# Cross attention's values computed at the start of a two-layer kernel and kept in DRAM, in place of beside the norm ahead of the queries

## The chip, the cores and the metric

The kernel runs on one core of a Trainium2 chip. The metric is the device time in microseconds (us), the median of several executions. The engines are called PE (TensorE), DVE (VectorE), ACT (ScalarE), POOL (GpSimd) and SP (SyncE, which here only issues DMAs).

## The reference, cut to what matters

Two layers with a conditioning vector, and then a block with its own weights. Its cross attention reads a memory `mem` of 256 tokens by 1024 features that depends on nothing computed before:

```
m  = rms_norm(mem, norm_mem)               # 256 x 1024
kv = m @ w_xkv                             # keys, values: 1024 features each
q  = rms_norm(x, norm_xattn) @ w_xq        # x: 256 latent tokens after the mixing layer
q, k normalised per head of 256 (4 heads), softmax(q k^T), times v, then w_xo, added to x
```

The norm divides every token's row by a root mean square r of that row. So the values of a token are `(mem * norm_mem) @ w_v / r`: the division may come before the product or after it.

The first layer needs `norm(x) * (1 + scale) + shift`, and scale and shift come from a product of the conditioning vectors with the ada weights; so the first feed-forward (called mlp00) can't begin before eight 1 MB pieces of `w_ada` have come and been used.

## The kernel before, in words

Activations stand feature-major: 128 partitions of features, tokens along the free dimension. Every large product is done in fp32r in three matmuls (`three`, L231): both operands are split into a high part and a low part, and lo*hi, hi*lo and hi*hi are added in PSUM. The weights come as 554 units of 128 x 1024 values (512 KB). For each unit SP issues a DMA into one of 3 landing buffers (`load`), ACT copies the high part into one of 4 slots (`feed_act`, L208), POOL subtracts to get the low part (`feed_pool`, L220), and PE uses it. SP's load of unit u waits for the low part of unit u-3, ACT's copy of u for PE's last use of u-4. The order of the units is the list `STREAMS`; the order of everything on an engine is the order in which its program is written, by hand, and semaphores count the steps (`mark`, `after`).

The start (`start_pe`, `start_act`, `start_dve`): PE does the eight ada pieces (`ada_pe`, each 8 products in 4 column groups), ACT squares the tokens (`square_act`, L636), PE sums the squares with a matrix of ones (`stat_pe`, L642), ACT takes the root (L690), DVE the reciprocal, PE spreads it over the partitions (`spread_pe`, L701), DVE multiplies (L729), ACT and DVE split into high and low (L715, L736). SP's order of DMAs: cond_pack, ada 0 and 1, tokens (2 MB), weight units 0 to 2, ada 2 to 7, then units from 3.

Much later the SSD heads run (`ssd_heads_*`): a loop over 16 heads in which PE, ACT, DVE and POOL alternate and PE does the products of conv_out besides. In its steps 11 to 18 ACT also squares one tile of the memory and PE sums it (`mem_square`, `mem_stat`, L2479). Their root and reciprocal go along with those of the SSD norm. In `ssd_out_*` the memory is multiplied by gain and reciprocal and split into mem_hi and mem_lo. Then follow the keys (`cross_k_pe`), the mixing product (`mix_pe`), and `cross_vq_pe`: the values (16 tiles of two 512-column products, 96 matmuls in all), with the sums and the spread of the norm of xattn written between them, and then the queries. The steps of that norm on ACT, DVE and POOL (L690, L729, L715, L763) lie beside the values' matmuls. `QUIET` names the norms in whose gaps no filler matmuls (`busy_pe`, L650) are put. Last come the attention heads (`cross_heads_*`), the output product and the last feed-forward (mlp_up, mlp_down).

During mlp00 ACT issues DMAs of further ada rows (`rows_dma`, L606), which DVE multiplies.

Of the kernel before, what the change touches and what calls it, by code (L numbers as in the profile page):

```python
# [51 lines left out]
class Feed:  # L52
# [12 lines left out]
    def ahead(self, stream, tiles):  # L65
# [6 lines left out]
                  ("ones", (128,))],  # L72
# [6 lines left out]
             ("norm_xattn", (8,)), ("norm_mem", (8,)), ("xattn_gains", (4,)), ("norm_mlp", (8,))],  # L79
}  # L80

STREAMS = ["w_up00", "w_down00", "w_dn", "w_dn_out", "w_up01", "w_down01", "w_up10", "w_down10",
           "w_swa_k", "w_swa_v", "w_swa_q", "w_swa_out", "w_up11", "w_down11",
           "w_glu", "w_gate", "w_k", "w_v", "w_q", "w_z", "w_dt", "w_xbc", "w_attn_out", "w_conv_out", "w_ssd_out", "w_xk", "w_mix",
           "w_xv", "w_xq", "w_xo", "w_mlp_up", "w_mlp_down"]
# [9 lines left out]
class Kit:  # L95
    def __init__(self, nc, ctx, dram, steps, counted):
# [10 lines left out]
        self.mem_landed, self.skewed, self.stored = sem("mem_landed"), sem("skewed"), sem("stored")  # L107
        f = lambda name, *shape, dtype=F32: ctx.enter_context(nc.sbuf_tensor(name, [P, *shape], dtype))
# [17 lines left out]
        self.rms, self.rr = f("rms", 96), f("rr", 96)  # L126
# [11 lines left out]
    def places(self):  # L138
# [12 lines left out]
        self.pieces = f("ada_pieces", 132, 256)  # L151

# [45 lines left out]
        self.mem_sq = f("mem_squares", 13, 2, LAT)  # L198
# [429 lines left out]


def square_act(k, act, st, d, src, ready):  # L630
    tokens = src.shape[-1]
    if ready is not None:
        act.wait_ge(*ready)
    if d >= 2:
        act.wait_ge(*k.PE.after(st, "stat", d - 2))
    k.nc.scalar.activation(k.sq[:, d % 2, 0:tokens], src, ACT.Square).then_inc(*k.AC.mark((st, "sq", d)))  # L636


def stat_pe(k, pe, st, d, tokens, bank=4):
    pe.wait_ge(*k.AC.after(st, "sq", d))  # L640
    for c in range(tokens // P):
        mm = k.nc.tensor.matmul(ck(k.B[bank], c), k.sq[:, d % 2, c * P:(c + 1) * P], k.C["ones"],  # L642
                                start=d == 0 and c == 0, stop=d == KT - 1, skip_group_check=True)
    mm.then_inc(*k.PE.mark((st, "stat", d)))
# [30 lines left out]

def sums_dve(k, dve, st, d, tokens):
# [3 lines left out]
    s, bank = k.sqs[:, 0:tokens], k.B[6 if st == "norm xattn" else 7][:, 0:tokens]  # L680
# [98 lines left out]
def up_freed(k, st):  # L779
    return lambda n: None if n < 4 else (k.DV.after(st, "raw", (n - 4) // 2) if n % 2 else k.AC.after(st, "silu", (n - 4) // 2))  # L780
# [1651 lines left out]
MEM_SQUARES = 10  # L2432
# [3 lines left out]
def ssd_heads_pe(k, pe):  # L2436
# [38 lines left out]
    def mem_stat(d):  # L2475
        pe.wait_ge(*k.AC.after("mem", "sq", d))
        for c in range(2):
            at = 288 + 2 * d + c
            mm = nc.tensor.matmul(k.B[5][:, at:at + 1], k.mem_sq[:, d % 2, blk(c)], k.C["ones"][:, 0:1], start=True, stop=True)  # L2479
        mm.then_inc(*k.PE.mark(("mem", "stat", d)))  # L2480

    for j in range(INNER + 4):
# [8 lines left out]
        if MEM_SQUARES < j <= MEM_SQUARES + KT:  # L2491
            mem_stat(j - 1 - MEM_SQUARES)
# [6 lines left out]
def ssd_heads_act(k, act):  # L2499
# [20 lines left out]
    def mem_square(d):  # L2520
        if d == 0:
            act.wait_ge(k.mem_landed, 16)
        if d >= 2:
            act.wait_ge(*k.PE.after("mem", "stat", d - 2))
        nc.scalar.activation(k.mem_sq[:, d % 2, :], k.mem[:, d, :], ACT.Square).then_inc(*k.AC.mark(("mem", "sq", d)))

    for j in range(INNER + 3):
# [10 lines left out]
        if MEM_SQUARES <= j < MEM_SQUARES + KT:  # L2538
# [948 lines left out]
```

## Time and profile before

| | before |
|---|---|
| median of 3 runs | 2796.22 us (2790.86 to 2797.05) |
| profiled execution, span from first to last instruction | 2797.4 us |
| PE busy | 2734.1 us, 98% |
| PE weight loads | 2393.1 us, 86% |
| DVE busy | 1431.5 us, 51% |
| ACT busy | 1184.1 us, 42% |
| POOL busy | 1470.3 us, 53% |
| mean granted clock of PE | 0.987 |

The profile gives no time of the profiled execution besides its span, so the span stands for it. The page also has the span in 40 slices of 70 us: PE is at 9 tenths or more in all but the first, which has 7. PEclk is the clock that was granted to PE, as a share of 2.4 GHz.

### The profile page before, as it was taken

The numbers are of one execution on the slowest core, as the hardware profiler recorded it, in microseconds if no ns is written. First come the engines' busy times: TensorE is split into PE (matmuls) and PEld (weight loads), VectorE is DVE, ScalarE is ACT, GpSimd is POOL, SyncE is SP. The second block draws the span as 40 slices with busy tenths as digits, with TensorE's granted clock in tenths as the row PEclk, the third lists the DMA queues.
The fourth block names the chain that finished last, engine by engine and source line by source line (L and its number), as shares of the span: only waits on it lengthen the run. The fifth ranks groups of instructions, "written<-read, shape, count | busy, mean of one in ns | idle before, by whom it ended". The sixth has DMA issues, their size and how long they took to land.

```text
span 2797.4 us, 52973 instructions
## 1 busy us (share of the span) xinstructions
PE 2734.1 (98%) x22044; PEld 2393.1 (86%) x22044; DVE 1431.5 (51%) x2755; ACT 1184.1 (42%) x2115; POOL 1470.3 (53%) x809
## 2 busy tenths in 40 slices
PE   7999999999999999999999999999999999999999
PEld 5888888778888888889888896899997898998999
DVE  3777327656654566415666035453184776612560
ACT  3222235335554322223222246544455565555553
POOL 2444434443324444444444442488884576696887
PEclk9999999999999999999999999999998999999999
DMA  6555322310002555434554336365563353354555
GB/s 263 200 200 196 120 90 90 94 46 4 4 26 68 189 181 179 129 98 147 181 187 155 105 96 129 99 196 186 173 188 109 107 157 123 111 177 136 156 190 160
DMA packets 105973, 380.96 MB, mean 136 GB/s; under 512 B 11367, under 2 KB 16648, under 8 KB 104456
## 3 DMA queue, kind: packets, MB, share of 16 engines
q1 hardware_dynamic: 87304, 310.47, 35.5%
q10 hardware_dynamic: 18432, 67.12, 6.9%
q8 instruction: 175, 2.87, 0.4%
q14 instruction: 62, 0.51, 0.1%
HBM read 373.34 MB, written 4.19 MB: 135 GB/s over the span
## 4 chain that ended last, share of the span: by engine, by line
PE 93%; ACT 3%; DVE 2%; issue 1%; POOL 1%; DMA 0%; SPq 0%; ACTq 0%; POOLq 0%
PE bank L233 26%; PE bank L234 25%; PE bank L235 25%; PE bank L1096 2%; PE upper_banks L234 1%; PE upper_banks L1898 1%; PE upper_banks L235 1%; PE upper_banks L233 1%; PE upper_banks L1881 1%; PE bank L1872 1%; PE upper_banks L1073 1%; PE upper_banks L1223 1%; PE bank L1210 1%; PE bank L1106 1%; PE upper_banks L1221 1%
## 5 line engine op out<-in xcount | busy, mean ns | idle before, releaser
L226 POOL TENSOR_TENSOR weights_lo<-weights_landing,weights_hi 128x1024 fp32r<-128x1024 f32 x554 | 1336.5, 2418 | 1175.9 <-ACT weights_hi L216 1175.2
L216 ACT ACTIVATE weights_hi<-weights_landing 128x1024 fp32r<-128x1024 f32 x554 | 587.1, 1061 | 1156.1 <-PE bank L235 1043.0
L233 PE MATMUL bank<-normed_hi,weights_lo 128*128 128x256 f32 (+1 forms) x2776 | 925.2, 333 | 3.4 <-DVE normed_lo L736 2.1
L234 PE MATMUL bank<-normed_lo,weights_hi 128*128 128x256 f32 (+1 forms) x2776 | 918.0, 331 | 0.0
L235 PE MATMUL bank<-normed_hi,weights_hi 128*128 128x256 f32 (+1 forms) x2776 | 917.0, 330 | 0.0
L233 PEld LDWEIGHTS bank<-normed_hi,weights_lo 128*128 128x128 f32 x2776 | 521.6, 188 | 70.0 <-issue 4.4
L235 PEld LDWEIGHTS bank<-normed_hi,weights_hi 128*128 128x128 f32 x2776 | 521.6, 188 | 56.1
L234 PEld LDWEIGHTS bank<-normed_lo,weights_hi 128*128 128x128 f32 x2776 | 521.8, 188 | 55.7
L233 PE MATMUL bank<-hidden_hi,weights_lo 128*128 128x256 f32 (+1 forms) x1026 | 340.5, 332 | 0.0
L234 PE MATMUL bank<-hidden_lo,weights_hi 128*128 128x256 f32 (+1 forms) x1026 | 340.5, 332 | 0.0
L235 PE MATMUL bank<-hidden_hi,weights_hi 128*128 128x256 f32 (+1 forms) x1026 | 340.0, 331 | 0.0
L818 DVE TENSOR_TENSOR hidden_lo<-silus,hidden_hi 128x512 fp32r<-128x512 f32 (+1 forms) x88 | 201.6, 2291 | 88.4 <-ACT hidden_hi L805 88.4
L234 PEld LDWEIGHTS bank<-hidden_lo,weights_hi 128*128 128x128 f32 x1026 | 192.6, 188 | 21.5
L233 PEld LDWEIGHTS bank<-hidden_hi,weights_lo 128*128 128x128 f32 x1026 | 192.6, 188 | 21.2
L235 PEld LDWEIGHTS bank<-hidden_hi,weights_hi 128*128 128x128 f32 x1026 | 192.6, 188 | 21.1
L872 DVE SCALAR_TENSOR_TENSOR residual<-bank,gate,residual 128x256 f32<-128x256 f32 x70 | 31.1, 479 | 331.8 <-PE bank L235 331.8
L620 DVE CUSTOM_DVE_ANT_0 ada_products<-ada_rows,upper_banks,k_cond_pack 128x1024 f32<-128x1024 f32 x128 | 163.2, 1275 | 22.6 <-DMA ada_rows<-w_ada_rows 13.4
L620 DVE CUSTOM_DVE_ANT_0 ada_rows<-ada_rows,upper_banks,k_cond_pack 128x1024 f32<-128x1024 f32 x128 | 163.2, 1275 | 0.0
L816 DVE TENSOR_TENSOR silus<-silus,bank 128x512 f32<-128x512 f32 (+1 forms) x88 | 54.6, 621 | 186.8 <-PE bank L235 151.9
L2111 DVE SCALAR_TENSOR_TENSOR upper_banks<-gl,k_pack,upper_banks 128x255 f32<-128x255 f32 (+14 forms) x240 | 113.4, 473 | 8.2
L867 DVE TENSOR_TENSOR residual<-residual,bank 128x256 f32<-128x256 f32 x24 | 9.9, 417 | 129.8 <-PE bank L235 129.8
L1014 DVE SCALAR_TENSOR_TENSOR dn_convs<-bank,k_pack,dn_convs 128x508 f32<-128x508 f32 (+1 forms) x96 | 71.8, 748 | 3.4
(465 smaller groups left out, 3687.2 us busy)
## 6 DMA issues: line engine op xcount, KB each, us to landing
weights_landing<-w_up SPq DMA_DIRECT2D x176, 512.0 KB, 3.5
ada_rows<-w_ada_rows ACTq DMA_DIRECT2D x128, 512.0 KB, 4.3
weights_landing<-w_down SPq DMA_DIRECT2D x88, 512.0 KB, 3.5
weights_landing<-w_dn SPq DMA_DIRECT2D x33, 512.0 KB, 3.5
weights_landing<-w_mlp_up SPq DMA_DIRECT2D x32, 512.0 KB, 3.5
weights_landing<-w_mlp_down SPq DMA_DIRECT2D x32, 512.0 KB, 3.5
weights_landing<-w_gate SPq DMA_DIRECT2D x24, 512.0 KB, 3.5
weights_landing<-w_xbc SPq DMA_DIRECT2D x24, 512.0 KB, 3.5
```

The lines of the kernel that those rows point to most:

```text
L216: k.nc.scalar.activation(k.WH[:, u % SLOTS, :], k.W[:, u % LANDS, :], ACT.Copy).then_inc(*k.AC.mark(("unit hi", u)))
L226: k.nc.gpsimd.tensor_tensor(k.WL[:, u % SLOTS, :], k.W[:, u % LANDS, :], k.WH[:, u % SLOTS, :].bitcast(F32), ALU.subtract).then_inc(*k.PO. ...
L233: nc.tensor.matmul(out, ll, rh, start=start, stop=False, skip_group_check=True)
L234: nc.tensor.matmul(out, lh, rl, start=False, stop=False, skip_group_check=True)
L235: return nc.tensor.matmul(out, lh, rh, start=False, stop=stop, skip_group_check=True)
L620: nc.vector.tensor_tensor_reduce(k.row[r % ROW_LANDS][:] if c else k.row_out[:], k.row[r % ROW_LANDS][:], k.upper[:, c * D:(c + 1) * D], 1 ...
L816: nc.vector.tensor_tensor(s, s, k.B[(2 * p + 1) % 4][:, 0:tokens], ALU.mult).then_inc(*k.DV.mark((st, "raw", p)))
L818: nc.vector.tensor_tensor(lo(p), s, hi(p).bitcast(F32), ALU.subtract).then_inc(*k.DV.mark((st, "lo", p)))
L872: nc.vector.scalar_tensor_tensor(x, k.B[n % 4][:, a - first:b - first], gate(n, c), x, ALU.mult, ALU.add).then_inc(*k.DV.mark(*([(st, "ev" ...
L1014: nc.vector.scalar_tensor_tensor(y[:, :, a:b], x[:, :, a + shift:b + shift], taps[:, j:j + 1], y[:, :, a:b], ALU.mult, ALU.add).then_inc(* ...
L1096: mm = k.nc.tensor.matmul(bank[block(to), at + c * BLK:at + (c + 1) * BLK], lhs(rows, to, c), rhs(rows, to, c), start=True, stop=True)
L2111: nc.vector.scalar_tensor_tensor(y[:, a:LAT], x[:, 0:LAT - a], w[:, at, j:j + 1], y[:, a:LAT], ALU.mult, ALU.add).then_inc(*k.DV.mark(("co ...
```

## The change

1. The unit stream `w_xv` goes from behind `w_mix` to the very front of `STREAMS`. A copy of the memory is loaded at the start, multiplied by norm_mem (not divided by the root), split in high and low, and the values' products are done between the ada pieces. Squares, sums and root of the memory are done there too. The division by the root is in the eviction from PSUM (`early_v_act`).
2. The values (1 MB) are stored into a DRAM tensor, and loaded again on SP ahead of the second unit of w_xq. ACT's first row DMA of mlp00 waits for the store, since it writes over that place.
3. The memory's statistics leave the SSD heads; the reciprocals `mem_r` kept from the start are used instead. The memory itself is still loaded again for the keys.
4. The tokens' squares at the start are summed by DVE in a bank (`sums_act`, `sums_dve`, `sums_pe`) instead of by 32 matmul blocks on PE (`stat_pe`).
5. The cross stage has no values in it: sums, spread, queries follow on the mixing product directly. `cross_spread_pe` comes after the third tile of the queries instead of the second. The keys' loop is written by tile, in the same order as before.

```diff
-STREAMS = ["w_up00", "w_down00", "w_dn", "w_dn_out", "w_up01", "w_down01", "w_up10", "w_down10",
+STREAMS = ["w_xv", "w_up00", "w_down00", "w_dn", "w_dn_out", "w_up01", "w_down01", "w_up10", "w_down10",
...
+    if st == "mlp00" and p == 0:
+        act.wait_ge(k.v_stored, 16)
...
-        if MEM_SQUARES < j <= MEM_SQUARES + KT:
-            mem_stat(j - 1 - MEM_SQUARES)
...
-        if MEM_SQUARES <= j < MEM_SQUARES + KT:
-            mem_square(j - MEM_SQUARES)
...
-def cross_vq_pe(k, pe):
...
-            if t == 2:
-                sums_pe(k, pe, "norm xattn", LAT)
-            if t == 6:
-                spread_pe(k, pe, "norm xattn", LAT)
-            wv = tile_parts(k, pe, "w_xv", t, 512)
...
+def cross_kq_pe(k, pe):
+
+    sums_pe(k, pe, "norm xattn", LAT)
+    spread_pe(k, pe, "norm xattn", LAT)
     linear(k, pe, "cross q", "w_xq", KT, KT, both2(k), LAT,
-           lambda n: k.AC.after("cross q", "ev", n - 4) if n >= 4 else k.AC.after("cross v", n // 2, n % 2), norm_ready(k, "norm xattn"),
+           lambda n: k.AC.after("cross q", "ev", n - 4) if n >= 4 else k.DV.after("mix", "ev", 4 + n), norm_ready(k, "norm xattn"),
            first=1, beside=lambda n: cross_beside_pe(k, pe, n))
...
+        if x == 0:
+            pe.wait_ge(k.v_loaded, 16)
...
+def early_v_pe(k, pe, u):
+
+    for t in (2 * u, 2 * u + 1):
+        e, d = t // KT, t % KT
+        wv = tile_parts(k, pe, "w_xv", t, 512)
+        if e == 0:
+            pe.wait_ge(*k.DV.after("early mem", "lo", d))
+        for c in range(2):
+            mm = three(k.nc, k.B[2 * e + c][:], [x[:, d, blk(c)] for x in (k.em_hi, k.em_lo)], wv, d == 0, d == KT - 1)
...
 def start_pe(k, pe):
     pe.wait_ge(*k.AC.after("cond"))
+    for u in range(3):
+        early_v_pe(k, pe, u)
+    ada_pe(k, pe, 0)
+    early_v_pe(k, pe, 3)
+    early_stat_pe(k, pe)
+    for u in range(1, 4):
         ada_pe(k, pe, u)
+        early_v_pe(k, pe, 3 + u)
+    ada_turn_pe(k, pe, 3)
+    early_v_pe(k, pe, 7)
+    sums_pe(k, pe, "norm00", TOK)
+    ada_pe(k, pe, 4)
+    spread_pe(k, pe, "norm00", TOK)
+    for u in range(5, ADA_FIRST):
+        ada_pe(k, pe, u)
     ada_turn_pe(k, pe, ADA_FIRST - 1)
...
+def early_v_act(k, act, e):
+    act.wait_ge(*k.PE.after("early v", e))
+    if e == 0:
+        act.wait_ge(*k.DV.after("early mem", "r"))
+    for c in range(2):
+        k.nc.scalar.activation(k.early_v[:, c, e * 512:(e + 1) * 512], k.B[2 * e + c][:], ACT.Identity,
+                               scale=k.mem_r[:, c:c + 1]).then_inc(*k.AC.mark(("early v", e, c)))
...
 def start_act(k, act):
...
+    for d in range(KT):
+        if d % 2 == 0:
+            feed_act(k, act, min(d // 2 + 1, LANDS))
+        if d == 0:
+            act.wait_ge(k.early_mem_landed, 16)
+        nc.scalar.activation(k.em_hi[:, d, :], k.early_mem[:, d, :], ACT.Identity, scale=k.C["norm_mem"][:, d:d + 1]).then_inc(
+            *k.AC.mark(("early mem", "hi", d)))
+    for d in range(KT):
+        nc.scalar.activation(k.early_sq[:, d, :], k.early_mem[:, d, :], ACT.Square).then_inc(*k.AC.mark(("early mem", "sq", d)))
+    feed_act(k, act, 5)
+    act.wait_ge(*k.DV.after("early mem", "sums"))
+    nc.scalar.activation(k.rms[:, 60:62], k.rms[:, 62:64], ACT.Sqrt, scale=1.0 / D, bias=k.C["eps"]).then_inc(*k.AC.mark(("early mem", "rms")))
+    early_v_act(k, act, 0)
+    feed_act(k, act, 7)
+    for u in range(4):
         ada_act(k, act, u)
-    act.wait_ge(k.tokens_landed, 16)
+    feed_act(k, act, 8)
     for d in range(KT):
-        square_act(k, act, "norm00", d, k.X[:, d, :], None)
+        sums_act(k, act, "norm00", d, k.X[:, d, :], (k.tokens_landed, 16))
     rms_act(k, act, "norm00", TOK)
-    feed_act(k, act, LANDS)
-    for u in range(2, ADA_FIRST):
+    early_v_act(k, act, 1)
+    feed_act(k, act, k.F.base["w_up00"] + LANDS)
+    for u in range(4, ADA_FIRST):
         ada_act(k, act, u)
...
+            F.base["w_up00"] + 6: values_out, F.base["w_xq"] + 1: values_in}
     sp.dma_start(k.C["cond_pack"][:], dram["cond_pack"]).then_inc(k.cond_landed, 16)
-    for u in range(2):
+    load(0)
+    sp.dma_start(k.early_mem[:], dram["late_mem"]).then_inc(k.early_mem_landed, 16)
+    load(1)
+    load(2)
+    for u in range(4):
         ada_dma(k, sp, u)
+        load(3 + u)
     sp.dma_start(k.X[:], dram["tokens"]).then_inc(k.tokens_landed, 16)
-    for u in range(LANDS):
-        load(u)
-    for u in range(2, ADA_FIRST):
-        ada_dma(k, sp, u)
-    for u in range(LANDS, len(F.source)):
+    load(7)
+    ada_dma(k, sp, 4)
+    ada_dma(k, sp, 5)
+    load(8)
+    ada_dma(k, sp, 6)
+    ada_dma(k, sp, 7)
+    for u in range(9, len(F.source)):
```

## Rows read from the trace of the kernel before

**Rows 1.** The page: its span, and the chain of waits by engine.

```profile
span 2797.4 us, 52973 instructions
...
PE 93%; ACT 3%; DVE 2%; issue 1%; POOL 1%; DMA 0%; SPq 0%; ACTq 0%; POOLq 0%
```

**Rows 2.** Timeline of the start (us, us, engine, line, names, count, [idle <-releaser]).

```profile
6.43 1.93 PE L521 MATMUL upper_banks<-ada_first,cond 128*32 128x256 f32 x16 [6.43 <-DMA ada_first<-w_ada]
...
24.11 1.07 PE L521 MATMUL upper_banks<-ada_first,cond 128*32 128x256 f32 x16
...
24.45 2.94 ACT L216 ACTIVATE weights_hi<-weights_landing 128x1024 fp32r<-128x1024 f32 x3
...
25.57 7.02 POOL L226 TENSOR_TENSOR weights_lo<-weights_landing,weights_hi 128x1024 fp32r<-128x1024 f32 x3 [25.13 <-ACT weights_hi L216]
...
30.34 6.35 DVE L729 SCALAR_TENSOR_TENSOR norm_work<-residual,scale,upper_banks 128x256 f32<-128x256 f32 x16
...
33.83 1.07 PE L521 MATMUL upper_banks<-ada_first,cond 128*32 128x256 f32 x16 [1.43 <-DMA ada_first<-w_ada]
...
38.30 0.80 PE L233 MATMUL bank<-normed_hi,weights_lo 128*128 128x512 f32 x1 [2.10 <-DVE normed_lo L736]
...
38.89 0.63 PE L234 MATMUL bank<-normed_lo,weights_hi 128*128 128x512 f32 x1
...
39.32 0.63 PE L235 MATMUL bank<-normed_hi,weights_hi 128*128 128x512 f32 x1
...
55.70 1.35 ACTq L606 DMA_DIRECT2D ada_rows<-w_ada_rows  x3
```

**Rows 3.** Windows: stretch, length, busy PE, PEld, DVE, ACT, POOL, PEclk, DMA share, GB/s.

```profile
32.00:34.00 2.00, 0.57 (x12) 0.16 (x8) 2.00 (x6) 0.00 (x0) 0.59 (x1) 1.00 1.04 420
...
42.00:44.00 2.00, 2.00 (x9) 1.59 (x8) 1.84 (x5) 2.00 (x5) 0.00 (x0) 0.79 0.00 0
```

**Rows 4.** Timeline of PE: first two matmuls of the values, first of the queries.

```profile
2514.41 0.39 PE L233 MATMUL bank<-weights_hi,mem_lo 128*128 128x512 f32 x1
2514.64 0.40 PE L234 MATMUL bank<-weights_lo,mem_hi 128*128 128x512 f32 x1
...
2538.39 0.28 PE L233 MATMUL bank<-normed_hi,weights_lo 128*128 128x256 f32 x1
```

**Rows 5.** Timeline beside the values: POOL's low parts of the norm, ACT's evictions.

```profile
2527.47 5.61 POOL L763 TENSOR_TENSOR normed_lo<-norm_work,normed_hi 128x256 fp32r<-128x256 f32 x8
...
2542.20 1.06 ACT L2799 ACTIVATE cross_v<-bank 128x512 f32<-128x512 f32 x2
```

**Rows 6.** Timeline of the norm between the cross output and mlp up.

```profile
2608.33 0.60 PE L659 MATMUL upper_banks<-k_cond_pack,square_sums 128*128 128x128 f32 x4
...
2609.42 1.28 ACT L690 ACT_TABLE_LOAD   x1
2609.45 0.71 PE L659 MATMUL upper_banks<-k_cond_pack,squares 128*128 128x128 f32 x4
...
2613.49 0.38 PE L233 MATMUL bank<-normed_hi,weights_lo 128*128 128x256 f32 x1
```

**Rows 7.** Timeline of the SSD heads: memory statistic, next work, two waits at the end.

```profile
2379.50 0.58 PE L2479 MATMUL upper_banks<-k_cond_pack,mem_squares 128*128 128x1 f32 x4
2379.95 0.47 PE L2454 MATMUL upper_banks<-ssd_xe,ssd_btok 128*128 128x128 f32 x2
...
2408.54 0.38 PE L233 MATMUL bank<-cv_hi,weights_lo 128*128 128x256 f32 x1 [0.39 <-DVE merged L2190]
...
2414.05 0.42 ACT L2518 ACTIVATE squares<-ssd_z 128x256 f32<-128x256 f32 x1 [0.67 <-POOL ssd_z L2605]
```

**Rows 8.** Instructions of square_sums (ns min/median/max, first to last); DMA issues (KB, us).

```profile
L682 DVE TENSOR_TENSOR upper_banks<-square_sums,squares x8: 699/1736/2116, 321.2 to 2599.1; 128x512 f32<-128x512 f32 x4, 128x256 f32<-128x256 f32 x4
...
skew<-by_dist SPq DMA_DIRECT2D x1, 3072.0 KB, 33.8
```

More of the change, by code:

```diff
@@ L625, in rows_dve @@
             ada_whole_dve(k, dve, r // KT)
[L630 to L644, printed above, removed]
 def busy_pe(k, n, bank=6):
@@ L2473, in stat @@
         mm.then_inc(*k.PE.mark(("ssd", "stat", j)))
[L2475 to L2480, printed above, removed]
     for j in range(INNER + 4):
@@ L2685, in ln_pool, with cross_k_tile_pe @@
         k.nc.gpsimd.tensor_tensor(k.cv_lo[:, d, :], k.cv[:, d, :], k.cv_hi[:, d, :].bitcast(F32), ALU.subtract).then_inc(*k.PO.mark(("ln", "lo", d)))
-def cross_k_pe(k, pe):
-    mem = lambda d: (k.mem_hi[:, d, :], k.mem_lo[:, d, :])
-    linear(k, pe, "cross k", "w_xk", KT, KT, mem, LAT,
-           lambda n: k.AC.after("cross k", "ev", n - 4) if n >= 4 else k.DV.after("ssd out", "add", 4 + n),
-           lambda d: k.PO.after("mem", "lo", d),
-           beside=lambda n: cross_stat_pe(k, pe, "cross k", n - 2) if n >= 2 else None)
+def cross_k_tile_pe(k, pe, n):
+    pe.wait_ge(*(k.DV.after("ssd out", "add", 4 + n) if n < 4 else k.AC.after("cross k", "ev", n - 4)))
+    for d in range(KT):
+        if n == 0:
+            pe.wait_ge(*k.PO.after("mem", "lo", d))
+        mm = three(k.nc, k.B[n % 4][:, 0:LAT], tile_parts(k, pe, "w_xk", n * KT + d), (k.mem_hi[:, d, :], k.mem_lo[:, d, :]), d == 0, d == KT - 1)
+    mm.then_inc(*k.PE.mark(("unit used", k.F.unit("w_xk", n * KT)), ("cross k", "acc", n)))
+def cross_k_pe(k, pe):
+    for n in range(KT):
+        cross_k_tile_pe(k, pe, n)
+        if n >= 2:
+            cross_stat_pe(k, pe, "cross k", n - 2)
 def mix_pe(k, pe):
@@ L3038, in start_pe, with early_stat_pe @@
+def early_stat_pe(k, pe):
+    for d in range(KT):
+        pe.wait_ge(*k.AC.after("early mem", "sq", d))
+        for c in range(2):
+            at = 32 + 2 * d + c
+            mm = k.nc.tensor.matmul(k.B[7][:, at:at + 1], k.early_sq[:, d, blk(c)], k.C["ones"][:, 0:1], start=True, stop=True)
+    mm.then_inc(*k.PE.mark(("early mem", "stat")))
 def start_pe(k, pe):
     pe.wait_ge(*k.AC.after("cond"))
-    for u in range(ADA_FIRST):
-        ada_pe(k, pe, u)
-        if u:
-            ada_turn_pe(k, pe, u - 1)
-        if u == 1:
-            for d in range(KT):
-                stat_pe(k, pe, "norm00", d, TOK)
-        if u == 2:
-            spread_pe(k, pe, "norm00", TOK)
@@ L3071, in start_dve @@
+    dve.wait_ge(*k.PE.after("early mem", "stat"))
+    nc.vector.reduce_sum(k.rms[:, 62:64], k.B[7][:, 32:48].rearrange("p (d c) -> p c d", c=2), AX_X).then_inc(*k.DV.mark(("early mem", "sums")))
+    dve.wait_ge(*k.AC.after("early mem", "rms"))
+    nc.vector.reciprocal(k.mem_r[:], k.rms[:, 60:62]).then_inc(*k.DV.mark(("early mem", "r")))
+    for d in range(1, KT - 1):
+        sums_dve(k, dve, "norm00", d, TOK)
+        if d == 3:
+            ada_dve(k, dve, 3)
     norm_r_dve(k, dve, "norm00", TOK)
-    ada_dve(k, dve, 3)
@@ L3252, in load, with values_out, values_in @@
         sp.dma_start(k.W[:, u % LANDS, :], F.source[u]).then_inc(k.landed[u % LANDS], 16)
+    def values_out():
+        sp.wait_ge(*k.AC.after("early v", 1, 1))
+        sp.dma_start(values, k.early_v[:]).then_inc(k.v_stored, 16)
+    def values_in():
+        sp.wait_ge(k.v_stored, 16)
+        sp.wait_ge(*k.PE.after("ssd out", "acc", KT - 1))
+        sp.dma_start(k.xv[:], values).then_inc(k.v_loaded, 16)
     def level():
```

99 lines of the change are left out of this document (42 added, 57 removed).

## The prediction

> **What bounds the kernel now.** I read the page's busy shares and chain first: the span is 2797.4 us and the chain of waits that ended last is 93% TensorE, so TensorE's queue is the path and any other engine counts only where it makes that queue wait [rows 1]. Then I looked for the places where the queue does wait in the stages that the change touches, by timelines and windows.
> *The start.* Until 38.30 us TensorE has almost no work: the 16-instruction groups of `ada_pe` follow the landing of the 1 MB pieces of w_ada, and the last of them waits 1.43 us for its DMA at 33.83 [rows 2]. In that time the queues move some 420 GB/s [rows 3]; so the start is bound by 12.4 MB of transfers. DVE's scaling, begun at 30.34, ends at 36.69, and the first matmul of mlp00 comes at 38.30 [rows 2], 1.61 us later. That matmul runs at TensorE's lower level: 512-column matmuls start 0.43 us apart (38.89 to 39.32) [rows 2], against 0.23 in the values' stage [rows 4], and the granted clock is still 0.79 in 42 to 44 us, so the 1.2 GHz level lasts to about 42.7 [rows 3].
> *The values.* The 96 matmuls of w_xv begin at 2514.41, those of cross q at 2538.39 [rows 4]: 23.98 us, all busy. Under them lies the whole norm of xattn.
> *The SSD heads.* Eight steps have a memory statistic of four passes each (`mem_stat`); the first group begins at 2379.50 and the next work at 2379.95, so 0.45 us [rows 7].
>
> **The change part by part.**
> *1. Values out of the cross stage.* Removed: 23.98 us. What is late next is the chain that lay beneath: residual, square, sums, root, reciprocal, spread, scale, hi, lo. The same chain, uncovered, stands between cross out and mlp up: from the first sums group at 2608.33 (right behind the last product) to the first matmul at 2613.49, 5.16 us [rows 6]. In it the root waits for a table load that ends at 2610.70, where its sums, begun 2609.45, would be ready near 2610.1 [rows 6]; the last table that this part of the program loads before xattn is already that of the root, so I take off 0.6: 4.56 us, and cross q begins at 2514.41 + 4.56 = 2518.97. Its first tile needs all eight low parts, which GpSimd makes in 5.61 us, 0.70 each [rows 5], against 0.35 for three matmuls of 256 columns (half of 0.233 [rows 4] each). So the first tile ends at 2518.97 + 7 x 0.70 + 0.35 = 2524.2; before it ended at 2538.39 + 24 x 0.117 = 2541.2. Gain **17.0 us**. The other seven tiles are as they were: one unit of weights each, 2.8 us on TensorE against 2.34 on GpSimd and 0.98 on ACT (7.02 and 2.94 for three) [rows 2]; three units of w_xq are converted before the norm, as before of w_xv. Bounds: 19 if the low parts go faster than the chain suggests, 13.5 if the clock falls (below).
> *2. The load of the values* (1 MB, on SP ahead of the second unit of w_xq). Queued behind it: that unit and the rest. 1 MB at 420 GB/s is 2.5 us; the unit is needed at 2524, some 20 us after its issue. Cost 0, and up to 2.5 if that cover were gone. The first output waits for it 25 us after its landing: 0. The cross_k spread moves by one tile of q; its reader, the scaling of keys, is needed only at the heads: 0.
> *3. Memory statistics out of the SSD heads.* Eight times 0.45, 3.6 in all. Not all on the path: the matmul at 2408.54 waits 0.39 us for `merged`, whose chain does not hold the statistic, and at the end the square at 2414.05 waits 0.67 for GpSimd's product, past two more [rows 7]. So 3 of 8 are hidden; 5 x 0.45 = 2.25, and one small root and one reduction less in the tail, 0.2 by estimate: gain **2.4 us** (bounds 0 and 3.8). The wait for mem moves from ACT to DVE 40 us later: 0. The keys' edit only splits `linear` into the same tiles in the same order, with the same statistics in the mix: 0; that "keys ahead of the mixing" is already so before.
> *4. The start.* Added transfers ahead of the last w_ada piece: mem, 1.05 MB, and nine weight units where there were three, 3.15 MB: 16.6 MB for 12.4. SP queues them with waits for "unit lo", but at every such wait some 2 MB stand in the queue, so it does not run dry. 4.2 MB more at 420 GB/s is +10 us: the lower bound, if transfers alone bind.
> Now the engines (us; each by the rows given). The first piece of w_ada (1.39 MB with what is ahead of it) is used at 6.43 [rows 2], so at 420 GB/s the bytes flow from 3.1. Landings in the new order: w_xv 0 at 5.2, mem 7.7, units 1 and 2 at 8.9 and 10.1, tokens at 30. ACT makes hi of unit 0, then the memory's hi (0.4 each, an estimate from DVE's halves, 6.35 for 16 [rows 2]) with units 1 and 2 between, squares (0.3 to 0.42 [rows 7]), unit 3 by 16.9; GpSimd's low parts (2.34 each) are ready at 8.7, 12.4, 14.8, 19.4 [rows 2]. TensorE: 8.9 first matmul; 10 of the 12 of a unit at 0.43, then 0.233 [rows 2, 4]: unit 0 to 13.7, units 1 and 2 (2.8 each) to 19.3, ada 0 (1.07) to 20.4 [rows 2], unit 3 to 23.2, then 8 statistics of 0.45 [rows 7] to 26.8. Behind these ACT waits: sums, root, reciprocal to 27.7, two evictions of 0.53 [rows 5] to 28.9, and only then hi of units 5 and 6 (0.98 each) to 30.9; low parts 5 and 6 at 32.3 and 34.7. TensorE: ada 1, unit 4, ada 2 to 31.8, **waits** to 32.3, unit 5, ada 3 to 36.2, unit 6 to 39.0. ACT waits for ada 3: piece and hi of unit 7 to 37.7, and only now the tokens' squares, though they landed at 30. Low part 7 is ready at 40.1 and unit 7 ends at 43.0. DVE adds the squares: first at 38.8, six sums of 0.70 [rows 8] with 0.05 between, and ada_dve(3), two small steps, for which I allow twice the square's 0.42 [rows 7], to 44.0. Sums on TensorE, twice 4 blocks at 0.22 (the 0.60 of two blocks holds some 0.16 of latency [rows 6]), to 45.8; root and reciprocal to 46.5; ada 4 and the spread (4 blocks, 0.7 by the same pace) to 47.4. DVE scales 16 halves in 6.35 [rows 2] to 53.75, beside which ada 5 to 7 land and pass (ACT's second evictions and three hi, to 50.2, before the last piece, 51.1). From there to the first matmul 1.61 again: **55.4**, against 38.30: **+17.1 us**. The clock is low there as before, since TensorE again idles over 3 us ahead of it.
> The upper bound is +22: were units 0 to 2 wholly at 0.43, 36 x 0.195 = 7.0 us are lost where I have 2.0.
> *5. The store of the values.* SP issues it behind w_up00's sixth unit, so after low part 10, near 55.5; ACT's first row DMA, which now waits for it, came at 55.70 [rows 2], 17.4 us after the first matmul, so near 72.8. At 420 GB/s it is done by 59: 0.
> *6. Clock in the new gap.* Between 2514.4 and 2519 TensorE has only the sums and the spread, some 1.2 us of work, and no filler (`QUIET`). If the clock falls to 1.2 GHz, three matmuls take 0.64 us, still under the low parts' 0.70 [rows 5], so the first tile hides it; I put **+0.5** for what reaches the second tile (0 to 3.5: 3.5 is 30 matmuls at 0.117 extra).
> Here a page speaks more sharply against the change. By the Trainium skill, "TensorE: Matmul & The Clock Gate", Part 1, low clock is the default and only sustained activity lifts it, so work put into a start full of waits is done cold. The row agrees for the first matmuls (0.43 apart at 38.89); which of the V units this strikes no row of before shows; that is rival B.
> **Sum:** 17.1 - 17.0 - 2.4 + 0.5 = -1.8 us. The profiled execution would go from 2797.4 to 2795.6; it stands 1.2 over the median of the runs, 2796.22, so the median becomes **2794.4**.
>
> **Rivals.** 0.2% is 5.6 us, about what a measurement of this kernel can tell from no change.
> *A, the start is bound by transfers only.* +10 in place of +17.1: -8.9, 2787.3. For it: 420 GB/s without a break to 34 us [rows 3]. Against it: the waits of ACT on the statistics and on ada 3 stand in the queue's order, 5 and 5 us long by rows; it needs them to be hidden.
> *B, V in the cold.* Units 0 to 2 at 0.43 and the statistics' one-column matmuls letting the clock fall again: +4.5 at the start, and the new gap 2 more: -1.8 + 6.5 = +4.7, 2801; with a little more it is a slower kernel. It decides when the first units need over 5 us each (the point: unit 2's end after 22 us). For: 0.43 us from 38.89 on; against: TensorE had idled before that, and here it works on from 8.9.
> *C, the store is slow.* A store to DRAM in the trace (3 MB to `skew`, rows of 1.5 KB) took 33.8 us [rows 8]. Were the values like it, ACT would stand at the first row DMA from 72.8 to 89, and with the four slots of weights about 6 us of slack: +10, 2804 (slower). It decides above 17 us from issue to landing. Against: rows of 8 KB here, and a third of the bytes, 11 us by that rate.
>
> **How the numbers follow.** Forecast 0.46 (0.38 within 0.2%, 0.03 faster, 0.05 slower), A 0.26 (0.22 faster, 0.04 within), B 0.22 (0.05 within, 0.17 slower), C 0.06 slower. Faster 0.25, within 0.47, slower 0.28. The range goes from A (2787.3) to C (2804), 2787 to 2804; the forecast's own is 2790 to 2799.
>
> **What would show it.** First matmul of mlp00 at 55.4 (A: 48.5; B: 60); ACT waiting for the early sums near 17 to 27 and for ada 3 to 36; first matmul of cross q 4.6 us behind mix; its first tile 5.2 us long, ended by GpSimd; periods of the heads at their end 0.45 shorter; no wait on v_stored or v_loaded. The prediction is wrong if the start grows by under 13 or over 21 us, or if some middle stage moves by over 1 us.

## The result, and the profile after

| | before | after |
|---|---|---|
| median of the runs, us | 2793.54 (4 runs, 2789.87 to 2797.05) | 2776.84 (4 runs, 2773.74 to 2783.19) |
| ratio, 95% interval | | 0.9942 [0.9929, 0.9956] |
| span of the profiled execution, us | 2797.4 | 2781.3 |

The changed kernel is 0.6% faster, where 2794.4 and a range of 2787 to 2804 stood in the forecast. For the profiled execution of before only the span is known; that of after, 2783.19 us long, has one 1.9 us shorter, so spans are held against spans here. The page after, to be held against [rows 1]:

```profile
span 2781.3 us, 52919 instructions
...
PE 91%; ACT 3%; DVE 3%; issue 1%; POOL 1%; DMA 0%; SPq 0%; ACTq 0%; DVEq 0%; POOLq 0%
```

TensorE is still the path, so the difference can be followed along its queue. The table gives the time of the first matmul of each stage in both traces, and how far the changed kernel is behind (+) or ahead (-).

| first matmul of | before | after | after - before | gained or lost since the row above |
|---|---|---|---|---|
| mlp00 | 38.30 | 60.25 | +21.95 | +21.95 |
| window attention's heads | 1701.67 | 1700.45 | -1.22 | **-23.17** |
| its output product | 1765.50 | 1769.66 | +4.17 | +5.39 |
| state-space heads | 2320.53 | 2321.22 | +0.68 | -3.49 |
| cross k | 2465.41 | 2465.50 | +0.10 | -0.58 |
| cross heads | 2564.31 | 2548.02 | -16.29 | -16.39 |
| the last matmul | 2794.39 | 2778.30 | -16.08 | +0.21 |

The cross stage gives what was forecast, the start costs more, and the largest gain of all lies between 60 and 1700 us, where the diff changes no matmul. Of the 3.49 us between the output product and the state-space heads, 5.38 belong to the second attention's heads (45.84 us before, 40.46 after); against it stand 1.9 lost elsewhere. The 5.38 are no effect of the change: the mean granted clock in that stage was 0.70 in the trace of before and 0.86 in that of after, but a second trace of the changed kernel has 44.97 us at 0.72, and two traces of one version of before (experiment 1, and once more beside experiment 13) have 43.20 and 41.20.

*The start.* Timelines of the start of the changed kernel, PE first, then ACT, POOL and DVE (start, length, engine, line, names, count, idle time and what ended it); they answer to [rows 2].

```profile
9.98 0.77 PE L236 MATMUL bank<-weights_hi,early_mem_lo 128*128 128x512 f32 x1 [9.98 <-DVE early_mem_lo L3089]
...
24.97 3.63 PE L3018 MATMUL upper_banks<-k_cond_pack,early_squares 128*128 128x1 f32 x32
28.53 1.34 PE L524 MATMUL upper_banks<-ada_first,cond 128*32 128x256 f32 x16
29.81 0.80 PE L236 MATMUL bank<-weights_hi,early_mem_lo 128*128 128x512 f32 x1
...
43.12 0.50 PE L236 MATMUL bank<-weights_hi,early_mem_lo 128*128 128x512 f32 x1 [0.65 <-POOL weights_lo L229]
...
47.78 1.16 PE L647 MATMUL upper_banks<-k_cond_pack,square_sums 128*128 128x128 f32 x8 [1.58 <-DVE square_sums L673]
...
60.25 0.77 PE L236 MATMUL bank<-normed_hi,weights_lo 128*128 128x512 f32 x1 [4.83 <-ACT normed_hi L706]
...
30.59 2.00 ACT L219 ACTIVATE weights_hi<-weights_landing 128x1024 fp32r<-128x1024 f32 x2
39.28 0.39 ACT L548 ACTIVATE ada_pieces<-upper_banks 128x256 f32<-128x256 f32 x1 [6.69 <-PE upper_banks L524]
...
31.72 4.74 POOL L229 TENSOR_TENSOR weights_lo<-weights_landing,weights_hi 128x1024 fp32r<-128x1024 f32 x2 [9.11 <-ACT weights_hi L219]
...
51.53 6.35 DVE L720 SCALAR_TENSOR_TENSOR norm_work<-residual,scale,upper_banks 128x256 f32<-128x256 f32 x16 [1.19 <-PE upper_banks L692]
```

It is the picture that step 4 drew: one-column sums to 28.6, GpSimd idle for 9.11 us because ACT held units 5 and 6 back until 30.59, ACT waiting 6.69 us for ada 3 and the tokens' squares behind that. It comes 4.85 us later than drawn. Windows of the same trace show one piece of it. The two rows are unit 3 and the slow first part of unit 4 of the values (stretch, length, busy PE, PEld, DVE, ACT, POOL, clock, DMA share, GB/s).

```profile
22.00:24.90 2.90, 2.90 (x16) 2.34 (x13) 0.00 (x0) 0.00 (x0) 0.61 (x1) 1.00 1.04 434
...
29.80:32.40 2.60, 2.60 (x10) 2.13 (x7) 0.00 (x0) 2.60 (x4) 0.68 (x1) 0.50 0.98 400
```

Behind the one-column sums the granted clock is 0.50, the lower of TensorE's two levels, though the engine had no idle time. The start of experiment 11 has the same sums 8 us later and no such stretch behind them, so the sums alone don't explain it.

*The middle.* Windows of 100 us inside mlp00, where every matmul has 512 columns: first before, then after.

```profile
100.00:200.00 100.00, 100.00 (x430) 80.31 (x430) 76.56 (x99) 27.53 (x36) 42.85 (x18) 1.00 0.61 208
```

```profile
100.00:200.00 100.00, 100.00 (x439) 82.05 (x438) 77.61 (x101) 28.35 (x36) 43.85 (x19) 1.00 0.58 203
```

TensorE is busy all the time at full clock in both, and yet does 439 matmuls in place of 430. The same instructions start 233.3 ns apart before and 228.9 after (means over the three feed-forwards that have 512 columns). Nothing waits; the matmul itself is faster by 2%. With some 5,200 such matmuls 4.4 ns come to 23 us, the whole of the -23.17.

*The cross stage* after, PE and POOL, to be held against [rows 4, 5].

```profile
2519.57 0.35 PE L236 MATMUL bank<-normed_hi,weights_lo 128*128 128x256 f32 x1 [1.87 <-DVE norm_work L720]
...
2524.70 0.28 PE L238 MATMUL bank<-normed_hi,weights_hi 128*128 128x256 f32 x1
...
2518.74 5.57 POOL L754 TENSOR_TENSOR normed_lo<-norm_work,normed_hi 128x256 fp32r<-128x256 f32 x8 [1.85 <-ACT normed_hi L2759]
```

The first query matmul starts 4.8 us behind the start of the mix's last product, and its tile lasts 5.2 us, paced by GpSimd's 0.70.

*A stall.* In window attention's heads, behind 13,443 matmuls of the program (as the trace counts them), TensorE stood 4.66 us for nothing that the profile shows, and started again at the lower clock:

```profile
1729.54 1.55 PE L1889 MATMUL upper_banks<-swa_pt,swa_v 128*64 128x128 f32 x11 [4.66 <-issue]
```

### The profile page after: what moved, and what is told of

The parts are those of the page before. It is cut to its first block, busy times and chain, and to the rows that moved or that the text cites. A ratio compares the mean times of both kernels' runs of the same rounds, so it can differ in the third digit from the quotient of the medians.

```text
span 2781.3 us, 52919 instructions
## 1 busy us (share of the span) xinstructions
PE 2706.5 (97%) x21996; PEld 2391.5 (86%) x21996; DVE 1446.7 (52%) x2770; ACT 1187.3 (43%) x2123; POOL 1474.2 (53%) x809
## 4 chain that ended last, share of the span: by engine, by line
PE 91%; ACT 3%; DVE 3%; issue 1%; POOL 1%; DMA 0%; SPq 0%; ACTq 0%; DVEq 0%; POOLq 0%
PE bank L236 25%; PE bank L238 25%; PE bank L237 25%; PE bank L1087 2%; PE upper_banks L238 1%; PE upper_banks L236 1%; PE upper_banks L237 1%; PE upper_banks L1889 1%; PE upper_banks L1872 1%; PE bank L1863 1%; PE upper_banks L1064 1%; PE bank L1201 1%; PE upper_banks L1103 1%; PE upper_banks L1212 1%; PE bank L1097 1%
```

## The experiments

Three theories for the middle were put down. **P, the place:** the change declares `mem_r`, 8 bytes, ahead of `region`, which is rounded up to 32 bytes; so all work tiles, which hold the activations that the matmuls read, start at byte 75200 of a partition where they started at 75168. The slots of the weights are declared earlier and stay. **Q:** TensorE's instruction stream, which the changed start has made another one. **R:** chance between executions.

**1. The kernel before, moved by 32 bytes.**

```
-        self.rms, self.rr = f("rms", 96), f("rr", 96)
+        self.rms, self.rr, self.spare = f("rms", 96), f("rr", 96), f("spare", 2)
```

> The kernel before with one unused SBUF tensor of 8 bytes per partition, so that every work tile behind it starts 32 bytes further on (at a multiple of 64 bytes from the partition's start, as in the changed kernel; before it is 32 past one). Theory P (placement): the changed kernel owes most of its gain to this shift, since its 512-column matmuls in the feed-forwards start 229 ns apart against 233; so this kernel loses some 26 us: 2767, and its trace shows the 229. Rival Q (the PE instruction stream's own position decides the 229): the stream is as before, so 2793.5 and 233. Rival R (chance of one execution): 2793.5 here, and the 229 may show up in any kernel or none.

Measured: 2771.09 us (2768.15 to 2773.89), ratio 0.9923 [0.9907, 0.9940]. Windows in mlp00 and in the last feed-forward (256 columns):

```profile
100.00:200.00 100.00, 100.00 (x438) 82.05 (x438) 77.00 (x100) 28.46 (x36) 44.64 (x19) 1.00 0.60 212
2640.00:2740.00 100.00, 100.00 (x851) 100.00 (x850) 39.62 (x37) 46.37 (x67) 85.28 (x36) 1.00 0.60 186
```

Eight unused bytes give the old kernel 19.2 us, more than the whole change gave (16.7, and 10.5 on this chip, experiment 3). The first matmul of window attention's heads comes at 1676.10 instead of 1701.67: 25.6 us.

**2. The changed kernel, moved by 32 bytes more** (`f("spare", 8)`, tiles at 75232).

> The changed kernel with 32 unused bytes added, so that its work tiles stand 32 past a multiple of 64 bytes, as in the kernel before. Theory P: it loses the 26 us that the shift gave and comes out some 10 us above the kernel before, near 2803, with 233 ns. Rival Q or R: as the changed kernel, 2777.

Measured: 2825.98 us (2819.85 to 2828.09), ratio 1.0120 [1.0105, 1.0135]. The gain of the middle was gone, as P says, but the size was missed: it is not the old place (96 in place of 32 over a multiple of 128), and it is a worse one.

**3. The changed kernel again**, beside them on that chip.

> The changed kernel itself, for the comparison on one chip. All theories: ratio 0.994 to the kernel before, near 2777, and 229 ns in the feed-forwards; rival R allows 233 ns and then 2800.

Measured: 2779.81 us (2775.26 to 2784.24), ratio 0.9958 [0.9942, 0.9973]. **At the same place the change costs 8.7 us**: 2779.81 against 2771.09.

**4. The kernel before with one matmul more at its start**, no byte moved.

```
+    busy_pe(k, 1, bank=5)
```

> The kernel before with one filler matmul more at the start of PE's program, hidden under the first DMAs, so that all PE instructions behind it stand one place further on. Theory P: 2793.5, 233 ns. Rival Q: the pace of the 512-column matmuls changes, between 226 and 236 ns, and the time with it, by up to 26 us.

Measured: 2791.71 us (2789.74 to 2802.43), ratio 1.0009 [0.9998, 1.0020], 431 matmuls in 100 to 200 us. Q falls, and not by this one displacement alone: experiment 1 has the faster pace with the old stream, experiment 2 the slower one with the new. R falls with experiments 1 and 3, whose counts repeat.

**5, 6, 7. Other places for the kernel before** (`f("spare", 10)`, `18` and `34`).

> The kernel before with 40 unused bytes, so that its work tiles start 64 bytes further than before (75232, 96 over a multiple of 128): the start that the changed kernel with 32 unused bytes had in an earlier run (2825.98 us). Theory (the place of the work tiles alone sets the pitch of the wide matmuls and costs what it costs in any kernel): the changed kernel lost 46 us from this start, so this one loses about as much against the kernel before shifted by 32 bytes (2771.09), 2810 to 2820 us, with the 512-column matmuls of the feed-forwards 231 to 237 ns apart. Rival (the place matters only through its distance to tiles that the change adds, or the slow run came from somewhere else in the changed kernel): 2771 to 2795 us.

> The kernel before with 72 unused bytes: its work tiles start at 75264, a multiple of 128, 64 bytes further than in the run at 2771.09 us. Theory with a period of 64 bytes: 2771 us (2766 to 2776), the 512-column matmuls 229 ns apart. Theory with a period of 128 bytes: another value, either side of it, over 5 us away. Rival (no rule in the place, each program falls where it falls): anything in 2765 to 2830 us.

> The kernel before with 136 unused bytes: its work tiles start at 75328, 128 bytes further than in the run at 2771.09 us (75200). Theory of a period of 128 bytes: 2771 us (2767 to 2775) and the 512-column matmuls 226, 229 and 232 ns apart by their operands, as there. Theory of another period: over 5 us away, as the starts at 75232 (2813.27) and 75264 (2803.13) were.

Measured: at 75232 2813.27 us, ratio 1.0080 [1.0065, 1.0095]; at 75264 2803.13 us, 1.0045 [1.0028, 1.0062]; at 75328 2783.76 us, 0.9972 [0.9946, 0.9997], but six runs from 2767.07 to 2798.67. The windows of the run at 75328, where the two widths part:

```profile
100.00:200.00 100.00, 100.00 (x430) 80.60 (x429) 76.30 (x99) 27.59 (x36) 43.34 (x18) 1.00 0.59 206
2640.00:2740.00 100.00, 100.00 (x885) 100.00 (x884) 44.43 (x37) 48.63 (x69) 93.30 (x39) 1.00 0.63 200
```

The counts of matmuls in those two windows for every place:

| work tiles at | 512 columns, 100 to 200 us | 256 columns, 2640 to 2740 us |
|---|---|---|
| 75168 (before, experiment 4) | 430, 431 | 852, 859 |
| 75200 (after, experiment 1) | 439, 438 | 851, 851 |
| 75232 (experiments 2, 5) | 430, 430 | 835, 835 |
| 75264 (experiment 6) | 432 | 845 |
| 75328 (experiment 7) | 430 | 885 |

Kernels with equal places agree within 1%: experiment 5 confirmed that 75232 is bad in either kernel, and every further trace with its tiles at 75200 (experiments 3 and 8 to 13) has 438 or 439 and 851 or 852. Both periods that I had proposed, 64 and 128 bytes, fell: 75264 and 75328 are slow for wide matmuls.

**8. The change without its start.** The diff's cross stage and heads, with the start of before. The values are not computed at all; a plain load of memory stands in their place.

```
-STREAMS = ["w_xv", "w_up00", ...
+STREAMS = ["w_up00", ...
-        sp.dma_start(k.xv[:], values)
+        sp.dma_start(k.xv[:]..., dram["late_mem"]...)
```

> The changed kernel with the start of the kernel before: the values of cross attention aren't computed (a plain load of memory takes their place, of the same size and at the same point) and memory's scale is left at 1; the rest is as in the changed kernel, with its work tiles at 75200. Left out: the values' 96 matmuls, their weights' 4 MB and memory's statistics. It isolates the two removals. By my steps 1 and 3: 17.0 and 2.4 us under the shifted kernel before (2771.09), 2751 to 2753 us, and 25 to 28 us under the changed kernel's repeat, nearly all of it at the first matmul of the first feed-forward. Rival (the cross stage gives back less, since the values also kept the clock and the low parts ahead): 2756 to 2762 us.

Measured: 2752.14 us (2751.11 to 2754.19), ratio 0.9864 [0.9850, 0.9878]: 18.95 under experiment 1, where steps 1 and 3 said 19.4, and 27.7 under experiment 3 (those two on another chip, where before stood at 2790.32 against 2791.04 here). The cross stage, from cross k to the cross heads, is 17.25 us shorter than in experiment 1.

**9. The heads' statistics alone left out** of experiment 1 (`mem_stat`, `mem_square` and their sums gone).

> The kernel before with its work tiles at 75200, with memory's squares and their sums left out of the state-space heads (memory is scaled by a wrong factor in their place, at the same cost). Step 3 of the prediction alone: 2.4 us under the shifted kernel before, 2768 to 2769 us, the heads' pitch 0.45 us shorter in 5 heads. Rival read from the two traces: 1 us or less, the pitch nearly the same, since another engine sets it.

Measured: 2771.37 us (2764.74 to 2774.64), ratio 0.9925 [0.9912, 0.9938]. In the medians nothing is to be seen, as the rival said. In the traces the way from the first state-space matmul to cross k is 2.9 us shorter than in experiment 1 (2.5 in experiment 8, 2.4 in experiment 3), but that way holds the output product too. The heads' periods say it more sharply: with the statistics four of them last 5.83 us, without them 5.43 here and 5.53 in the changed kernel. So four heads give 0.4 or 0.3 each, 1.2 to 1.6 us, where step 3 had five at 0.45; the rest of the 2.4 to 2.9 is not shown to be the statistics'.

**10 to 13. The start.** Is it the queues' order, or the transfers (rival A)? Four orders, nothing left out of any. In the first, ACT makes units 5 and 6 ahead of memory's root and squares the tokens ahead of the piece of ada 3:

```
-    feed_act(k, act, 5)
+    feed_act(k, act, 7)
     act.wait_ge(*k.DV.after("early mem", "sums"))
...
     early_v_act(k, act, 0)
-    feed_act(k, act, 7)
+    for d in range(KT):
+        sums_act(k, act, "norm00", d, k.X[:, d, :], (k.tokens_landed, 16))
+        if d == 2:
+            feed_act(k, act, 8)
     for u in range(4):
         ada_act(k, act, u)
-    feed_act(k, act, 8)
-    for d in range(KT):
-        sums_act(k, act, "norm00", d, k.X[:, d, :], (k.tokens_landed, 16))
     rms_act(k, act, "norm00", TOK)
```

> The changed kernel with three steps of its start moved, nothing left out: ScalarE makes the high parts of units 5 and 6 of the values' weights before it waits for memory's sums; it squares the tokens before it waits for ada product 3; TensorE sums the squares before the turn of ada 3 and unit 7. Theory Q (the 22 us that the start grew by are mostly this queue order: the sums, squares and scaling wait behind the values' work): the first matmul of the first feed-forward at 49 to 53 us instead of 61.25, and 2769 to 2773 us against the 2779.81 of the changed kernel's own repeat. Rival T (transfers or POOL's low parts set it): the first matmul not before 57 us, 2776 to 2780 us.

Measured: first matmul of mlp00 at 59.42; 2778.95 us (2774.35 to 2780.86), 0.9952 [0.9937, 0.9967]. A miss for theory Q: both numbers are the rival's. ACT had the squares done at 39.1, but TensorE stood behind its own work. Its window:

```profile
36.00:50.00 14.00, 14.00 (x105) 10.10 (x104) 3.21 (x7) 3.93 (x9) 2.00 (x1) 1.00 0.70 286
```

In the second, the statistics stand behind unit 5 as well:

> As the run with the reordered start, and the 32 one-column matmuls of memory's sums (4.87 us at 24.36 in the changed kernel's repeat, after which the clock fell and unit 4 of the values ran its first five matmuls 0.43 us apart) stand behind unit 5 of the values instead of behind unit 3. If the sums' place costs through the clock and the low parts' order: 1 to 3 us faster than the reordered start alone. Rival: they only fill waits for the low parts and the ada transfers, within 1 us of it; if memory's scale then holds ScalarE up ahead of the tokens' squares, 1 to 3 us slower.

Measured: first matmul at 61.88; 2780.44 us (2777.53 to 2784.14), 0.9961 [0.9946, 0.9975]. The rival's harm: ACT waited 7.87 us for memory's sums, and the tokens' squares began at 38.38 instead of 32.92. The third puts the tokens' load ahead of ada 2, two matmuls on squares summed by VectorE in place of 32, the tokens' sums and spread ahead of unit 6, and unit 7 last:

```
+    ada_pe(k, pe, 3)
+    sums_pe(k, pe, "norm00", TOK)
     ada_turn_pe(k, pe, 3)
...
     spread_pe(k, pe, "norm00", TOK)
-    for u in range(5, ADA_FIRST):
+    early_v_pe(k, pe, 6)
+    for u in range(4, ADA_FIRST):
         ada_pe(k, pe, u)
     ada_turn_pe(k, pe, ADA_FIRST - 1)
+    early_v_pe(k, pe, 7)
```

> The changed kernel with its start put in another order, nothing left out: memory's squares are summed over the tiles by VectorE and by 2 matmuls instead of 32; the tokens are loaded ahead of ada 2; their sums and the spread stand ahead of unit 6 of the values, and unit 7 stands behind the last ada product, while the normed tokens' parts are made; its evictions follow the norm. Theory Q' (TensorE's own order bounds the start: in the reordered start it had no wait between 36 and 50 us, and the tokens' sums stood ready 5 us before they were taken): the first matmul of the first feed-forward at 47 to 51 us instead of 61.25, 2767 to 2771 us. Rival T (the transfers, 5 MB more than before): not before 53 us, 2772 to 2776 us.

Measured: first matmul at 55.90; 2777.78 us (2777.54 to 2783.95), 0.9959 [0.9946, 0.9972]. A miss for Q' too: 5.35 us earlier than in experiment 3, but past the rival's 53, and slower than either range. Two rows of it, an ACT wait for unit 6 with the tokens' squares behind it, and a TensorE wait for unit 9's low part, which gave back 3 us:

```profile
32.32 1.06 ACT L219 ACTIVATE weights_hi<-weights_landing 128x1024 fp32r<-128x1024 f32 x1 [3.78 <-DMA weights_landing<-w_xv]
...
64.59 0.77 PE L236 MATMUL bank<-normed_hi,weights_lo 128*128 128x512 f32 x1 [3.02 <-POOL weights_lo L229]
```

The fourth takes both away:

```
     early_v_act(k, act, 0)
-    feed_act(k, act, 7)
+    for d in range(KT):
+        sums_act(k, act, "norm00", d, k.X[:, d, :], (k.tokens_landed, 16))
+        if d in (2, 4, 6):
+            feed_act(k, act, 5 + d // 2)
...
+        if d == 3:
+            feed_act(k, act, 10)
```

> The changed kernel with its start rebuilt further, nothing left out: tokens loaded right behind ada 1, ScalarE takes the eviction of the first half of the values and the tokens' squares before the high parts of units 5 to 7 (in the first rebuilt start it stood waiting for unit 6 until 32.32 us with the tokens there), and makes unit 9's high part between the normed ones (TensorE had waited 3.02 us for its low part). If the order is what is left: first matmul of the first feed-forward at 48 to 51 us and no wait of over 1 us behind it, 2765 to 2770 us, at or under the shifted kernel before. If the transfers set it (99% busy from 5 to 43 us in the first rebuilt start): 53 to 56 us, 2773 to 2777 us.

> The kernel before with 8 unused bytes once more (work tiles at 75200), for the comparison with the three kernels beside it on the same chip: 2771 us (2768 to 2774) if the place holds its gain from one chip and hour to another; a rival (the gain is of one chip) would give 2785 us or more.

Measured, on one chip: 2771.65 us (2763.03 to 2778.15), 0.9926 [0.9907, 0.9946], beside 2772.24 (2765.97 to 2778.16), 0.9927 [0.9907, 0.9946], for the shifted kernel before. The first matmul comes at 50.90, 10.35 earlier than in experiment 3 and as expected, with no wait behind it in 11 us and the clock at 1.00; the median is 1.7 above its range. The transfers ran full till 42:

```profile
5.00:42.00 37.00, 29.07 (x172) 21.13 (x173) 17.19 (x23) 22.46 (x39) 19.68 (x9) 1.00 1.01 414
50.90:62.00 11.10, 11.10 (x50) 9.06 (x49) 6.46 (x12) 8.95 (x17) 6.38 (x3) 1.00 0.22 51
```

So the order was half of what the start had cost, and with the best order found the change is worth nothing: +11.9 at the first matmul, +14.6 by cross k, and 16.4 back in the cross stage.

**14, 15. Each width at its own place.** The kernel before with its tiles at 75328, but the five tiles of the 512-column stages 128 bytes lower, at 75200, and the same with the fourth start:

```
+        if name in ("normed_hi", "normed_lo", "norm_work", "hidden_hi", "hidden_lo"):
+            offset -= 128
```

> The kernel before with the work tiles at 75328, but the five tiles that the 512-column stages read and write (normed high and low, the norm's work, hidden high and low) 128 bytes lower, where the run at 2771.09 us had them. Two readings from the profiles: at 75200 the 512-column matmuls start 227 to 230 ns apart and the 256-column ones 117.4; at 75328 233.3 and 113 to 114. Theory (each width's pitch goes by the place of its own tiles, and holds): both gains at once, 2748 to 2758 us. Rival (the 113.7 ns of the run at 75328 were of that execution alone, since its six runs went from 2767 to 2799 us): 2765 to 2780 us, wide apart.

> The rebuilt start of the run beside it with the split places of the other: if both hold and add up, 2743 to 2756 us, the fastest of all; if the split places don't hold, within 6 us of the rebuilt start alone (2765 to 2777 us).

Measured: 2754.44 us (2751.06 to 2757.82), ratio 0.9865 [0.9845, 0.9885], **the fastest version, faster than both kernels**; and with the new start 2760.52 us (2759.72 to 2762.45), 0.9888 [0.9869, 0.9906]. Windows of the first:

```profile
100.00:200.00 100.00, 100.00 (x438) 82.14 (x437) 76.67 (x100) 28.69 (x37) 44.60 (x19) 1.00 0.60 209
2640.00:2740.00 100.00, 100.00 (x884) 100.00 (x884) 28.26 (x27) 44.37 (x56) 90.62 (x38) 1.00 0.64 199
```

and the narrow one of the second, whose tiles lie at the same addresses:

```profile
2640.00:2740.00 100.00, 100.00 (x851) 100.00 (x850) 28.47 (x28) 44.30 (x57) 84.85 (x36) 1.00 0.59 188
```

Both gains came at once in the first, as the theory had it. The second fell between its two ranges: the wide gain held (438) and the narrow one did not in that stage. Two earlier windows, again of the first and then of the second, show that neither trace keeps one narrow pace:

```profile
1800.00:1900.00 100.00, 100.00 (x854) 100.00 (x853) 48.49 (x34) 47.98 (x70) 85.74 (x37) 1.00 0.61 189
2020.00:2080.00 60.00, 60.00 (x532) 60.00 (x531) 47.12 (x97) 32.20 (x45) 52.98 (x23) 1.00 0.64 194
```

```profile
1800.00:1900.00 100.00, 100.00 (x851) 100.00 (x851) 51.00 (x36) 48.55 (x72) 87.29 (x37) 1.00 0.62 191
2020.00:2080.00 60.00, 60.00 (x532) 60.00 (x531) 55.61 (x118) 31.77 (x46) 54.03 (x24) 1.00 0.62 196
```

The tiles at 75200 have 512 matmuls in 2020 to 2080 us (after, experiment 1), so 532 is the faster pace. With the narrow tiles at 75328 one and the same execution goes from the one pace to the other between stages, in both traces; together with the spread of experiment 7 this says that the narrow matmuls' pace has a second cause. It was not found.

## Why the prediction was wrong

The forecast was -1.8 us; the spans of the profiled executions show -16.1 and the medians -16.7. That the changed kernel is faster at all is owed to eight bytes that the forecast didn't look at: at equal place it is 8.7 us slower. Step by step:

*1. Values out of the cross stage*, -17.0: right. 4.6 us from the first sums to the first query matmul were said, 4.7 came, and 5.2 us for its tile were said and came; 16.4 in the traces of before and after, 17.25 in experiment 8.

*2, 5. The load and the store*: right at 0. The store took 7.9 us from issue to landing and ACT did not wait for it, so rival C falls; no row shows a wait for the load.

*3. Statistics out of the heads*, -2.4: too much. The periods show 1.2 to 1.6 us, from four heads and not five. Between before and after the heads are 1.2 us shorter and their output product 0.6 longer, which leaves the table's 0.58.

*6. The clock in the new gap*, +0.5: the queries' matmuls ran 0.21 us apart, at the lower level, from 2521.3 to 2524.3, and the low parts' 0.70 hid them. The mechanism is right; nothing reached the second tile, so the 0.5 was not needed.

*4. The start*, +17.1: mis-sized, 21.95 came, over the 21 that was to tell of a wrong forecast. It is just inside the bound of +22, but by luck: that bound was made of units 0 to 2 all at the lower clock, which did not come. The error is spread over the chain and each piece lengthens it: first matmul at 9.98 for 8.9 (+1.1); units 0 to 2 and ada 0 done at 22.07 for 20.4 (+0.6 more); unit 4 at the lower clock, 4.25 us for 2.8, of which unit 5, begun at 35.06 for 32.3, keeps +1.1; the squares' chain of ACT and DVE, their sums and the spread, scaling begun at 51.53 for 47.4 (+1.4 more); from its end to the first matmul 2.37 for 1.61 (+0.8). The slow unit 4 is the half of rival B that came true; units 0 to 2 were slow only to 15.2 us. The Trainium skill's rule that was weighed there ("TensorE: Matmul & The Clock Gate", Part 1, sustained activity lifts the clock) agrees with this trace in unit 0, whose matmuls start 0.43 us apart from 9.98 on. Rival A, transfers alone, is refuted for this order and is nearly what the fourth order reaches: +11.9 for its +10.

*The step that failed is one that the prediction didn't have.* It put every stage between mlp00 and the heads at nothing, and never costed the edit `self.mem_r = f("mem_r", 2)`. Those 8 bytes moved all work tiles by 32, and the 512-column matmuls went from 233.3 to 228.9 ns: 23.2 us, more than any step of the sum. Experiment 1 gives it without the change (25.6), experiment 2 takes it from the change, and between them they exclude the instruction stream, as experiment 4 does. Why the pace goes with the place stays open.

*The rest*, 5.4 us lost in window attention's heads, was in no step either. A stall of 4.3 to 4.7 us stands behind 13,443 matmuls in all five traces whose start has the changed kernel's matmuls (after, experiments 2, 3, 10 and 11). The three whose start has 28 fewer show 1.6 to 1.9 behind 13,442 (experiments 12, 13 and 15), experiment 4 2.0 behind 13,443; before has 0.9 behind 13,442, its moved versions 0 to 1.4, experiment 8 none. So where it stands goes with the count in TensorE's instruction stream, whatever instruction comes next; its size does not only, since two traces of one kernel (experiment 1 and the version beside experiment 13) have 0 and 1.1. After the long ones the clock is at 0.50, in after from 1729.5 to 1733. That instructions arrive late there is only argued: the DMA share is 0.93 in it, but 0.92 in before without a stall.

At equal place (experiment 3 against 1) the ledger closes without the middle: +22.9 start, -2.1 to window attention, +5.9 in it, +1.6 to the state-space heads (the stage whose clock varies from trace to trace has 1.8 of it), -2.4 heads and their output, -17.1 cross stage, +1.7 its heads and the rest: +10.6 at the last matmul, +8.7 in medians. My own sum for that was -1.8; the start and the stall are the difference.

## What to carry to other kernels

A tensor of a few bytes declared ahead of the work tiles is an edit of every matmul behind it: when a change adds one, note where the tiles start before and after, and compare the two versions at the same place, or its effect is read as the change's. Moving work into a start that is already full of transfers pays only what its own queue order leaves: here 24 us of matmuls cost 22 there, 12 in the best order found, and gave back 17. When a stage that the diff doesn't touch has moved, count its instructions per 100 us before looking for waits.

## What the runs showed of the hardware

- With TensorE busy all the time at the full clock, 512-column matmuls of the same shapes started 228.9 ns apart (work tiles at 75200), 233.3 (75168, 75232, 75328) or 232.7 (75264). At 75232 the three products of a step differ: 231, 232 and 237 ns. The 256-column ones averaged 113 to 120 ns in a stage, the slowest of their three products 122 (75232). With them at 75328 the average changes between 113 and 117.5 from stage to stage of one execution. Which of the tiles, or their distance to which other, does it is open.
- 32 one-column matmuls without a gap (3.63 us, clock 1.00) were followed by a stretch at 0.50, and in three further traces they were themselves slower at their end and followed by one (experiments 2, 3 and 10). In experiment 11 they took 3.63 us too, began at 32.76 instead of 24.97, and the clock stayed at 1.00. Where two took their place (experiments 12 and 13) the values' units behind them stayed at 0.23 us. So the stretch is not shown to follow from them alone.
- The stall behind 13,443 matmuls: up to 4.66 us in which TensorE waited for nothing that the profile shows.
